# Second row projection between the choice logits, and ScalarE adding up the comparisons of the two widest tiles in the threshold search

## The reference

```python
proj = x @ w_in + b_in                                   # 25 channel groups of 128, and 776 row columns
logits = einsum('bqhd,bsd->bqhs', iq, ik) * 64**-0.5     # 8 index heads
score = einsum('bqhs,bqh->bqs', relu(logits), iw * 8**-0.5)
score = where(admissible, score, -inf)
_, idx = top_k(score, 256)                               # the keys each query attends to
ya = gelu(a_u) * (W_s @ layer_norm(gelu(a_v)) + b_s)     # spatial gating
km, vm = split(mem @ w_mem_kv, 2)                        # keys and values of 256 memory tokens
```

## Time and profile before

| | us |
|---|---|
| median of 3 runs | 2799.52 |
| the profiled execution's own time | 2799.01 |
| its span (first to last instruction) | 2796.6 |
| PE busy / DVE busy / ACT busy | 2701.4 / 2102.8 / 1003.9 |
| choice logits | about 1134.9 to 1206.4 |
| second row projection | about 1206.4 to 1241.4 |
| memory tokens | about 1241.4 to 1258.2 |
| channels 7 to 24 with the gating's matmuls | about 1258.2 to 1462.2 |
| threshold search (31 rounds) | about 1211.3 to 1413.2 |
| ties | 1418.8 to 1457.6 |

### The profile page before, as it was taken

One profiled execution on the slowest core, in us unless ns is written; L12 is line 12 of the kernel. 1 busy time (PEld: TensorE's weight loads), 2 busy tenths in 40 slices (PEclk: granted clock), 3 DMA queues, 4 the chain that ended last, 5 costly groups with the idle time before them and its releaser, 6 DMA issues. The chain is left out here.

```text
span 2796.6 us, 33524 instructions
## 1 busy us (share of the span) xinstructions
PE 2701.4 (97%) x13192; PEld 2204.8 (79%) x13192; DVE 2102.8 (75%) x2852; ACT 1003.9 (36%) x1468; POOL 485.8 (17%) x260
## 2 busy tenths in 40 slices
PE   6999999999999989899999899999999999999998
PEld 5888888888888868588775578888878888888887
DVE  6999998874725672599986876698176988887978
ACT  5111112142413332412117651365232555455332
POOL 0000000000100001002220100345210566665000
PEclk9999999999999999999999999999999999999999
DMA  5212322223335542011110032110122222225431
GB/s 222 114 61 70 111 79 64 91 102 128 94 118 172 152 148 77 31 61 46 46 44 15 31 113 95 53 31 20 57 113 83 83 91 83 76 91 171 183 98 61
DMA packets 97566, 250.18 MB, mean 89 GB/s; under 512 B 7345, under 2 KB 34353, under 8 KB 95746
## 3 DMA queue, kind: packets, MB, share of 16 engines
q1 hardware_dynamic: 92866, 231.49, 24.3%
q10 hardware_dynamic: 4288, 15.73, 1.4%
q0 software_dynamic: 256, 0.82, 0.1%
HBM read 202.92 MB, written 45.09 MB: 89 GB/s over the span
## 5 line engine op out<-in xcount | busy, mean ns | idle before, releaser
L369 PE MATMUL pair<-u_hi,w_hi 128*128 128x512 f32 x768 | 302.1, 393 | 1.2 <-PEq L92 0.9
L640 DVE SCALAR_TENSOR_TENSOR conv_acc<-aT,cols,conv_acc 128x1024 f32<-128x1024 f32 x232 | 297.8, 1284 | 6.7
L370 PE MATMUL pair<-u_lo,w_hi 128*128 128x512 f32 x768 | 300.1, 391 | 0.0
L371 PE MATMUL pair<-u_hi,w_lo 128*128 128x512 f32 x768 | 299.9, 391 | 0.0
L369 PEld LDWEIGHTS pair<-u_hi,w_hi 128*128 128x128 f32 x768 | 145.1, 189 | 32.5 <-issue 2.4
L370 PEld LDWEIGHTS pair<-u_lo,w_hi 128*128 128x128 f32 x768 | 145.1, 189 | 30.7 <-issue 0.7
L1867 DVE TENSOR_SCALAR_CACHE_REDUCE counted<-choice,top_i 128x384 uint8<-128x384 f32 (+2 forms) x192 | 169.2, 941 | 0.0
L371 PEld LDWEIGHTS pair<-u_hi,w_lo 128*128 128x128 f32 x768 | 145.0, 189 | 30.5
L369 PE MATMUL pair<-h_hi,ch_hi 128*128 128x512 f32 x392 | 154.9, 395 | 2.2 <-ACT ch L1763 2.0
L370 PE MATMUL pair<-h_lo,ch_hi 128*128 128x512 f32 x392 | 152.7, 389 | 0.0
L371 PE MATMUL pair<-h_hi,ch_lo 128*128 128x512 f32 x392 | 152.6, 389 | 0.0
(11 more groups left out here) (497 smaller groups left out, 7001.0 us busy)
## 6 DMA issues: line engine op xcount, KB each, us to landing
wt<-in_w_ch SPq DMA_DIRECT2D x60, 512.0 KB, 3.5
wo_raw<-in_w_out SPq DMA_DIRECT2D x44, 512.0 KB, 3.6
wt<-in_w_up SPq DMA_DIRECT2D x10, 1024.0 KB, 4.9
w_raw<-in_w_up SPq DMA_DIRECT2D x10, 1024.0 KB, 4.8
g_spill<-g_stage SPq DMA_DIRECT2D x40, 256.0 KB, 2.2
ada_mod<-in_ada_mod SPq DMA_DIRECT2D x4, 2048.0 KB, 14.3
wt<-in_w_conv SPq DMA_DIRECT2D x16, 512.0 KB, 3.5
qk<-qk_st SPq DMA_DIRECT2D x8, 1024.0 KB, 6.6
```

What stands on the lines that cost most here:

```text
L369: nc.tensor.matmul(bank, w[0], x[0], start=(first and k == 0), stop=False)
L370: nc.tensor.matmul(bank, w[0], x[1], start=False, stop=False)
L371: return nc.tensor.matmul(bank, w[1], x[0], start=False, stop=(last and k == n_k - 1))
L640: nc.vector.scalar_tensor_tensor(dst, x, w, conv_acc[:], ALU.mult, ALU.add).then_inc(conv_step, 1)
```

## The change

**The second row projection moves between the logits.** Only channel 5 and the 8 pieces of the projection are now fill work: 80 steps, shared out by tile width plus one (`fill_share`). The pieces go to PSUM pair 3 in two alternating banks; the first waits until ACT has evacuated channel 5 from there, and from the third on each waits for DVE's evacuation two pieces back. Channel 6 stands after the logits. The weights' high part is made after relu 7 (it was 16), the low part after accumulation 8 (it was 18), channel 5 is evacuated after relu 15 (it was 33), and the evacuations of the pieces stand between DVE's accumulations. ACT's Gelu of a_v moves ahead of channel 6's evacuation. The load of channel 9's weights moves behind those of the memory tokens on SP.

**ACT counts the two widest tiles.** In a round DVE only compares tiles 7 and 6 (an instruction without a count, into `reached`, one byte an element), ACT copies each comparison onto itself with an accumulator (`sums`), and DVE counts the other four tiles. `sums_at` fixes which rounds stand where in ACT's order: rounds 1 to 4 around the memory tokens' evacuations, then before the wait for channel n: round 5 (n = 7), 6 and 7 (8), 8 (9), 9 (10), 10 (11), and two for each n from 12 to 21, rounds 29 and 30 standing before the wait for channel 21.

```diff
-        counted = at(13, "counted", [P, 2, S], mybir.dt.uint8)
+        counted = at(13, "counted", [P, 2, 6 * P], mybir.dt.uint8)
+        reached = [at(kb, f"reached{t}", [P, (t + 1) * P], mybir.dt.uint8) for t, kb in ((6, 19.0625), (7, 14.5))]
...
-        corner_set, counts_ok, step_ok, cand_ok, thr_ok, tie_step = (sem("top_" + x) for x in (
-            "corner", "counts", "step", "cand", "thr", "tie"))
+        corner_set, counts_ok, step_ok, cand_ok, thr_ok, tie_step, reach_ok, sums_ok = (sem("top_" + x) for x in (
+            "corner", "counts", "step", "cand", "thr", "tie", "reach", "sums"))
+        counts_upto = lambda n: 6 + 4 * (n - 1)
...
-        N_CH, LATE, FILL = len(channels), 21, (5, 6)
+        N_CH, LATE, FILL = len(channels), 21, 5
         SGU_AT = 19
-        CH_PAIR = [2, 0, 3, 1, 2, 3, 3] + [n % 4 for n in range(7, SGU_AT)] + [2, 3, 0, 1, 2, 3]
+        CH_PAIR = [2, 0, 3, 1, 2, 3, 0] + [n % 4 for n in range(7, SGU_AT)] + [2, 3, 0, 1, 2, 3]
+        FILL_STEPS = 2 * KT + KT * TT
+        fill_share = [sum(logits[m][0] + 2 for m in range(0, n + 1, 2)) for n in range(0, len(logits), 2)]
+
+        def filled(n):
+            return FILL_STEPS * fill_share[n // 2] // fill_share[-1]
+
+        def pair_that_ends(step):
+            return next(n for n in range(0, len(logits), 2) if filled(n) >= step)
+
+        FILL_TILE_AT = pair_that_ends(2 * KT) + 1
+        ROW_PIECE_AT = [pair_that_ends(2 * KT + KT * (j + 1)) + 1 for j in range(TT)]
...
             channel_weights(sp, 8)
-            channel_weights(sp, 9)
             sp.wait_ge(relu_ok, len(logits))
             sp.wait_ge(acc_ok, len(logits))
             sp.dma_start(mem_sb[:], a["mem"].rearrange("(m p) d -> p m d", p=P)).then_inc(mem_in, 16)
             sp.dma_start(w_km[:], a["w_km"].rearrange("o p k -> p o k")).then_inc(mem_in, 16)
             sp.dma_start(w_vm[:], a["w_vm"]).then_inc(mem_in, 16)
+            channel_weights(sp, 9)
...
-            def row_projection(step, n):
+            def row_step(bank, n, t, k):
                 c0, c1 = row_columns(n)
-                pe.wait_ge(row_lo, step + 1)
+                last = products(bank[:, 0:c1 - c0], [x[:, k, t * P:(t + 1) * P] for x in h2_parts],
+                                [w_row[n][i][:, k, :] for i in (0, 2)], k, KT)
+                if k == KT - 1:
+                    last.then_inc(row_mm, 1)
+
+            def first_rows():
+                pe.wait_ge(row_lo, 1)
                 for t in range(TT):
-                    j = step * TT + t
                     if t >= 4:
-                        pe.wait_ge(row_ok, j - 3)
-                    bank = row_bank(j)[:, 0:c1 - c0]
+                        pe.wait_ge(row_ok, t - 3)
                     for k in range(KT):
-                        last = products(bank, [x[:, k, t * P:(t + 1) * P] for x in h2_parts],
-                                 [w_row[n][i][:, k, :] for i in (0, 2)], k, KT)
-                    last.then_inc(row_mm, 1)
+                        row_step(row_bank(t), 1, t, k)
+
+            def fill_step(i):
+                if i < 2 * KT:
+                    channel_step(pe, FILL, i)
+                    return
+                t, k = divmod(i - 2 * KT, KT)
+                if t == 0 and k == 0:
+                    pe.wait_ge(row_lo, 2)
+                    pe.wait_ge(ch_out, FILL + 1)
+                if t >= 2 and k == 0:
+                    pe.wait_ge(row_ok, TT + t - 1)
+                row_step(pair[3][:, t % 2, :], 0, t, k)
...
-            row_projection(0, 1)
+            first_rows()
...
-                while at_fill < 4 * KT * (logit_cols[n // 2] - 6) // (logit_cols[-1] - 6):
-                    channel_step(pe, FILL[at_fill // (2 * KT)], at_fill % (2 * KT))
+                while at_fill < filled(n):
+                    fill_step(at_fill)
                     at_fill += 1
             pe.wait_ge(relu_ok, len(logits))
-            pe.wait_ge(ch_out, 7)
-            row_projection(1, 0)
+            for h in range(2):
+                channel(pe, FILL + 1, h)
...
+            def sums(first, end):
+                for b in range(first, end):
+                    for i, t in enumerate((7, 6)):
+                        act.wait_ge(reach_ok, 2 * b + i + 1)
+                        nc.scalar.activation(reached[t - 6][:], reached[t - 6][:], ACT.Copy,
+                                             accum_out=top_f[:, 0, t - 2:t - 1]).then_inc(sums_ok, 1)
+
+            ROW_HIGH_AT = 7
...
-                if n == 16:
+                if n == ROW_HIGH_AT:
                     row_high(1, 0)
-                if n == 33:
-                    act.wait_ge(ch_mm, 6)
+                if n == FILL_TILE_AT:
+                    evacuate(5)
                     channel_high(act, 7)
-                    evacuate(5)
+            act.wait_ge(row_ok, 2 * TT)
+            nc.scalar.activation(row2[:, :, 0:MEM], row2[:, :, 0:MEM], ACT.Gelu_apprx_tanh).then_inc(a_gelu, 1)
+            sums(0, 1)
...
+                if i in (0, 2):
+                    sums(i + 1 if i else 1, i + 3)
                 act.wait_ge(kv_mm, i + 1)
                 nc.scalar.activation((kmT if i < 2 else vm)[:, i % 2, :], pair[1 + i // 2][:, i % 2, 0:MEM],
                                      ACT.Copy).then_inc(kv_ok, 1)
-            act.wait_ge(row_ok, 2 * TT)
-            nc.scalar.activation(row2[:, :, 0:MEM], row2[:, :, 0:MEM], ACT.Gelu_apprx_tanh).then_inc(a_gelu, 1)
+            sums_at = [5, 6, 8, 9, 10] + [min(31, 2 * n - 11) for n in range(11, N_CH)] + [31]
             for n in range(7, N_CH):
+                sums(sums_at[n - 7], sums_at[n - 6])
...
-            ROWS_AT = [2, 4, 5, 6, 7, 9, 10, 11]
...
+                bank = pair[3][:, t % 2, :] if step else row_bank(t)
+                dve.wait_ge(row_mm, step * TT + t + 1)
+                nc.vector.tensor_tensor(row2[:, t, c0:c1], bank[:, 0:c1 - c0], b_row[:, c0:c1],
                                         ALU.add).then_inc(row_ok, 1)
...
-                w, at0 = (t + 1) * P, 6 * n + t - 2
+                w, at0 = (t + 1) * P, (counts_upto(n) if n else 0) + t - 2
                 if at0 >= 2:
                     dve.wait_ge(counts_ok, at0 - 1)
-                nc.vector.tensor_scalar(counted[:, t % 2, 0:w], scores(t), least, None, op, ALU.add,
+                to = counted[:, t % 2, 0:w] if t < 6 else reached[t - 6][:]
+                nc.vector.tensor_scalar(to, scores(t), least, None, op, ALU.add,
                                         accum_out=found[:, t - 2:t - 1]).then_inc(counts_ok, 1)
...
-                if n == 18:
+                if n == ROW_LOW_AT:
                     row_low(1, 0)
+                for t in range(TT):
+                    if n == ROW_PIECE_AT[t]:
+                        row_evacuation(1, t)
...
-                for t in range(2, TT):
+                for t in (7, 6):
+                    nc.vector.tensor_scalar(reached[t - 6][:], scores(t), cand[:, t - 2:t - 1].bitcast(F32), None,
+                                            ALU.is_ge).then_inc(reach_ok, 1)
+                for t in range(2, 6):
                     count(n + 1, t, cand[:, t - 2:t - 1].bitcast(F32), ALU.is_ge)
-                    if t in (4, TT - 1) and 2 * n + (t > 4) in ROWS_AT:
-                        row_evacuation(1, ROWS_AT.index(2 * n + (t > 4)))
-                dve.wait_ge(counts_ok, 6 * (n + 2))
+                dve.wait_ge(counts_ok, counts_upto(n + 2))
+                dve.wait_ge(sums_ok, 2 * (n + 1))
```

More of the change, by code:

```diff
@@ L1689, in mix_tensor @@
             at_fill = 0
-            logit_cols = [sum(logits[m][0] - 1 for m in range(0, n + 1, 2)) for n in range(0, len(logits), 2)]
             for n in range(0, len(logits), 2):
@@ L1825, in row_evacuation @@
                 c0, c1 = row_columns(1 - step)
-                j = step * TT + t
-                dve.wait_ge(row_mm, j + 1)
-                nc.vector.tensor_tensor(row2[:, t, c0:c1], row_bank(j)[:, 0:c1 - c0], b_row[:, c0:c1],
+                bank = pair[3][:, t % 2, :] if step else row_bank(t)
+                dve.wait_ge(row_mm, step * TT + t + 1)
+                nc.vector.tensor_tensor(row2[:, t, c0:c1], bank[:, 0:c1 - c0], b_row[:, c0:c1],
                                         ALU.add).then_inc(row_ok, 1)
@@ L1872, in mix_vector @@
             last.then_inc(bq_ok, 1)
+            ROW_LOW_AT = 8
             row_low(0, 1)
@@ L1933, in mix_vector @@
                 count(32, t, thr[:, t - 2:t - 1].bitcast(F32), ALU.is_gt)
-            dve.wait_ge(counts_ok, 6 * 33)
+            dve.wait_ge(counts_ok, counts_upto(32) + 6)
             nc.vector.tensor_scalar(room, found, -1.0, float(TOPK), ALU.mult, ALU.add).then_inc(tie_step, 1)
```

## The result

The changed kernel took 2805.4 us (median of 20 runs, 2798.84 to 2810.55) against 2799.81 (20 runs, 2797.73 to 2803.0): a ratio of 1.0018, 95% interval [1.0011, 1.0025]. It is slower by 5.6 us. The prediction was 2801.1, so the sign was right and the time 4.3 us too low, inside the range of 2794.5 to 2809 but just outside the likeliest case's, 2797 to 2805. The profiled execution took 2807.85, with a span of 2805.9 against 2796.6. It is the fifth slowest of the 20, while the profile before was taken in a run near its median. So the 9.3 us by which the spans differ are 3.7 more than the medians' 5.6, and what follows accounts for the two profiled runs.

The account below looks back on a forecast made before the run. TensorE was taken to set the stage's end, VectorE 7.5 us behind. Front -6.0 plus tail +7.6 gave +1.6 us, so 2801.1 us, with 8 in 10 within 2794.5 to 2809.

Parts of the forecast that it names:

- What bounds the kernel: Stage up to the first attention scores: TensorE sets its end, VectorE is 7.5 us behind, so a shorter search brings nothing.
- The front, -6.0: First logit to first memory product: 7.7 us gained by filled relu waits, 6.0 after one half-clock stretch is charged.
- I charge one stretch to the two in front: Waits for channel 5's bank and memory loads: together one half-clock stretch of 3.4 us, which takes 1.7.
- The bound of two stretches: Front, worse bound: two half-clock stretches behind its waits, leaving a gain of 4.3 us.
- The search, two rounds in 10.9 us: Beside the channels: the search goes at TensorE's pace, VectorE needs 4.8 us a round, and TensorE is not held up.
- rival D: In the search: the ScalarE part does nothing, comparisons stay at 1.27 us, one more microsecond in the tail, 2802; within forecast's 0.60.
- rival B: Channels: ScalarE falls behind as comparisons stay slow and POOL stops one per channel; 2820, or 2810 at half; chance 0.12.
- The tail, +7.6: Channel 20's end to first attention maximum: 54.0 us instead of 46.4, with TensorE waiting 6.1 us before channel 21.
- Either one alone keeps the tail at 54: Tail: TensorE's way (54.0 us) and VectorE's way (53.8) agree, so each by itself holds it there.
- After the first maximum all shifts together.: From the first attention maximum on: everything moves by the same amount, with no known wait in between.
- rival C: Whole kernel: three or more idle times with long half-clock stretches, such as one of 13.6 us, giving 2807; chance 0.12.
- A (tail cheap): Tail: wait before channel 21 covered or front better than its bound, 2793.8 with tail at 2; chance 0.16.

Follow-up runs that it names:

- e2: ScalarE sums alone, with their own list of rounds, on the kernel before, row projection left behind the logits: 2801.41 us, ratio 1.0004.
- f1: e3 plus 14 matmuls whose result nobody reads in TensorE's wait for the memory tokens' copies: 2796.14 us, ratio 0.9991.
- g2: f1 with the list of rounds fitted as in g1: 2793.2 us, ratio 0.9978.
- e1: The changed kernel without ScalarE sums, VectorE counting all six tiles, so the moved row projection alone: 2805.42 us, ratio 1.0019.
- e3: The whole change with the rounds' sums placed earlier in ScalarE's list: 2793.88 us, ratio 0.9977 to the kernel before.
- e4: The whole change with channels 21 to 24 in other banks, mg and mq changing places: 2801.94 us, ratio 1.0005.
- f3: e3 with channel 5 evacuated in two halves: 2792.06 us, ratio 0.9973.
- g3: e4 with POOL's final two multiplications held until the ties are over: 2797.08 us, ratio 0.9990.
- g4: e3 with the list of rounds fitted as in g1, the base for g1 and g2: 2793.85 us, ratio 0.9978.
- f4: e3 with the memory tokens' copies made first on ScalarE and channel 5 evacuated in halves: 2791.52 us, ratio 0.9975.
- g1: f4 with the list of rounds fitted to its earlier channels: 2788.19 us (5 runs), ratio 0.9953.

## Why the prediction was right, and where it was not

The forecast of +1.6 us was the sum of two terms that were both too favourable: the front gained 2.6 us less than forecast and the tail lost 3.7 more. In the profile that is +7.9 at the first maximum. The time stayed in the range (the profiled run's 2807.85 too) because 2 us of that did not reach the exponential, and because the range was wide. The mechanism, a front gained and a tail lost to VectorE and TensorE together, was right; the size was partly luck.

**What bounds the kernel.** Right: in the kernel before TensorE sets the end and VectorE has 7.5 us of slack. e2 shortened the search alone and gained nothing.

**The front, -6.0; it was -3.4 at channel 20's end.** The waits were found at their places: 3.0 us for channel 5's bank (2.9 reckoned), and 1238.05 for the first product (1236.7). The 1.35 us between them are the clock's: behind channel 5's wait lay a stretch of 3.4 us, after which channel 6 started at 1221.48 instead of 1219.9. The memory loads were no late matter: the last landed 8.8 us after its issue, not at 1233.8 but as channel 6 ended (1232.4), and TensorE waited for ScalarE alone, 3.6 us. The step that failed is "I charge one stretch to the two in front": both waits had one, and the second was 6.8 us long and cost 3.0. The bound of two stretches (a gain of 4.3) was passed because the prediction took a stretch to be 3.4 us long. f1 shows that the second comes of the wait: with 3.2 of the 3.6 us filled, and the products starting when they did, it is not there. g2 is the same; the seven profiles with 3.4 to 3.6 us unfilled at this place (the change, e1, e3, e4, f3, g3, g4) all have it.

**The search, two rounds in 10.9 us.** Right. A comparison without a count and with one-byte output is priced by the lower bound:

```profile
L1955 DVE TENSOR_SCALAR reached<-choice,top_i 128x1024 uint8<-128x1024 f32 x31 | 23.3, 753 | 0.0
```

That ends rival D: the prediction had no row for this comparison and chose between two bounds, and the chosen one was right. A round took 4.72 us (4.8 reckoned), VectorE waited 33 us for ScalarE, and TensorE was not held up between channels 7 and 20. POOL's subtraction stopped only one pair of comparisons in 31 (3.43 us, at 1233.63), so rival B's mechanism is there and its price in the rounds was 2 us in all.

**The tail, +7.6; it was +11.3** (1415.35 to 1473.01 is 57.7, before 46.4). The wait before channel 21 was 5.9 us (6.1 with its 0.2). TensorE's way came to the reckoned 54 and a little: 5.9, four channels, 2.0 of clock, to 1466.8, and 2.9. VectorE's way was right up to the ties (16.9 us behind channel 20's end, 10.3 + 6.65 reckoned; its own 5.7 and 4.8 make 10.5, and 10.2 was measured), and the ties are the term that was mis-sized: 40.9 us where 36.8 were reckoned. The prediction counted the two subtractions of POOL that meet them and left out that ties which end after channel 24 meet its multiplications too. Those cost two more stops of 2 us (3.25 for 1.29, 2.72 for 0.69). "Either one alone keeps the tail at 54" is wrong by that: VectorE's way was the longer by 3 us. e4, where TensorE waits for nothing before channel 21, still had its attention wait for VectorE, and g3 took two of the stops away.

The prediction also held that it is plain comparisons that are stopped. The instruction of 3.25 us is none: it reads the scores and the ties, two tensors. The Trainium skill (SBUF — State Buffer, Who interferes with whom) says that a VectorE instruction with two SBUF inputs contends with a GpSimd one that reads SBUF; by that rule the trace agrees. Of the six kinds of tie instruction four were seen stopped in these profiles (lines 1989, 1998 and 2000 of the changed kernel, and line 1951 of the kernel before: 2.37 us at 1420.21, for 0.42 unstopped). Some 2 us of the 7.9 by which the first maximum is late did not reach the exponential, which before had waited for ScalarE's table load behind four evacuations.

**"After the first maximum all shifts together."** Wrong in the profile: +5.8 at the first exponential became +9.3. No wait appears there that was not there before. The lower clock held for 20.5, 13.7 and 3.4 us in the attentions where it held for 13.7 and 10.2 before. But this part is not shown to be the change's. In e1's profile, whose tail is as late, the lower clock held there for 10.2 and 6.8 us only, and +8.3 at the first exponential (1475.95) became +5.9 at the end. These stretches differ from one profile to the next, and where the last 3.5 us of the changed kernel's profile come from stays open.

All runs, by the mean granted clock of each (the two columns are from two sets of runs):

| granted clock | changed kernel, mean us (runs) | before, beside e1 to e4 |
|---|---|---|
| 0.985 to 0.986 | 2809.5 (4) | none |
| 0.987 to 0.988 | 2805.8 (10) | none |
| 0.989 | 2802.2 (1) | 2803.2 (1) |
| 0.990 | 2800.9 (3) | 2801.4 (18) |
| 0.991 | 2799.1 (2) | 2798.8 (13) |
| 0.992 | none | 2797.7 (1) |

Where their clocks are equal the two kernels take about the same time, but only 6 of the changed kernel's 20 runs lie there, and the other 14 have a lower clock and are slower. That is what one would see if the waits bring more half-clock stretches and these make most of the 5.6 us, which is rival C's mechanism; its 2807 is nearer to the profiled run than the forecast is. The table sorts runs by an outcome and does not show it. Nor is the clock all: e3, whose front has the same two stretches, took 2794.2 in its five runs at 0.990, 6.7 us less than the changed kernel's three, of the 11.5 between the medians.

**The rivals.** A (tail cheap) is refuted for this order of the work, and e3 shows that it was one list away: the order on ScalarE "admits no other course" only as written. B did not occur. That TensorE's wait of 5.9 us would be there without the sums (e1) was nowhere in the prediction, which reckoned the search's later start only together with them.

## What to carry to other kernels

Moving work off a busy engine is worth what the order on the receiving engine lets through: here 33 us of VectorE waits came from the places of the sums in ScalarE's list, and a new list was worth 11.5 us. Such a list has to be fitted again when anything beside it gets faster: f4 was 7.2 us under the kernel before beside it, and g1, which is f4 with a fitted list, 11.5. Where two engines both end a stage, reckon each to its end with everything that runs beside it there, including what starts only when the other engine is done.

## What the hardware showed unexpectedly

A wait of 3.0 us in work that was full on both sides was followed by 3.4 us at 1.2 GHz, and waits of 3.6 and 5.9 us by 6.8 us each. The length of the wait does not settle it: e4, g3 and f3 had 3.4 us behind waits of 3.5, 3.6 and 3.4, and g2 and g3 none behind their 3.0. Nor is 3.0 the smallest: 2.0 us in e2 (at 1180.61, for channel 5's bank) and 1.9 in f3 were followed by 3.4 us at the lower clock, while the same 2.0 in the kernel before and the same 1.9 in f4 and g1 were not. Filling the wait of 3.6 us with 3.2 us of unread matmuls removed its stretch from two profiles of two, and the time of the whole did not fall (g2 against g4).

A copy of 1024 one-byte elements onto itself with an accumulator took ScalarE 1.04 us, about the 1.06 of a float32 instruction of the same shape without an accumulator (the high part of a channel's weights): the smaller element gained nothing there.
